# Sharing the last expert rows between two engines, and a new order of the first queries

## The reference

```python
def one_block(xb):                       # 128 tokens
    q = (xb @ wq).reshape(n, 8, 2, 64)                       # 8 heads of queries
    s = einsum('nhpk,pmk->nhpm', q, sub_keys)                # 2 x 128 scores per head
    sv, si = top_k(s, 16); cand_s = sv[0] + sv[1]; top_s, top_j = top_k(cand_s, 16)
    e = expert numbers of the 16 best;  g = softmax(top_s)
    act = gelu(einsum('nd,nhkd->nhk', xb, u[e]))             # u, v: 16384 rows of 1024 per layer
    return einsum('nhk,nhkd->nd', g * act, v[e])
```

## Time and profile before

| | us |
|---|---|
| median of three runs | 4258.71 |
| the three runs | 4248.27, 4258.71, 4259.67 |
| the profiled execution, its own time | 4255.55 |
| its span, first to last instruction | 4253.7 |
| PE busy / DVE / ACT / POOL in it | 3637.2 / 2550.2 / 963.9 / 2586.6 |
| moved by DMA | 1519.95 MB, 357 GB/s over the span |

### The profile page before, as it was taken

How to read it: one execution, slowest core, us unless ns; L and a number is a source line. 1 busy time by engine, 2 the same in 40 slices (tenths; PEclk the granted TensorE clock), 3 DMA queues, 4 the chain that set the end, 5 groups by cost and what they waited for, 6 DMA issues and landing times.

```text
span 4253.7 us, 37633 instructions
## 1 busy us (share of the span) xinstructions
PE 3637.2 (86%) x10554; PEld 1695.8 (40%) x10554; DVE 2550.2 (60%) x6442; ACT 963.9 (23%) x2490; POOL 2586.6 (61%) x2833
## 2 busy tenths in 40 slices
PE   7889899989988888888877899999898887777777
PEld 3354454545434223443332355554443432222222
DVE  1165456767665546566666555677676566666663
ACT  1212222222221112122222222222231122122121
POOL 0047446666665556676667663566676677777775
PEclk8899999999999999999999999999999999999999
DMA  6467889999999999999999988999999999999998
GB/s 240 160 237 270 283 325 391 360 392 403 361 366 383 376 383 354 351 362 351 400 396 409 354 291 298 364 369 389 394 407 350 368 401 406 407 406 405 401 402 325
DMA packets 472259, 1519.95 MB, mean 357 GB/s; under 512 B 59980, under 2 KB 78704, under 8 KB 471544
## 3 DMA queue, kind: packets, MB, share of 16 engines
q0 software_dynamic: 368640, 1342.34, 81.8%
q1 hardware_dynamic: 103416, 175.21, 11.6%
HBM read 1511.70 MB, written 5.67 MB: 357 GB/s over the span
## 4 chain that ended last, share of the span: by engine, by line
PE 44%; DMA 27%; POOL 13%; issue 9%; DVE 4%; ACT 2%; SPq 1%; DVEq 0%; ACTq 0%; POOLq 0%
PE expert_sum L2021 23%; DMA expert_rows<-in_peer_v,experts 23%; POOL expert_rows L989 11%; PE work L1780 4%; DMA expert_rows<-in_peer_u,experts 4%; PE work L1754 4%; PE work L1972 3%; PE work L1987 2%; PE work L1916 2%; PE work L1943 2%; PE work L1728 2%; DVE expert_rows L1697 1%; POOL stat_rstd L936 1%; PE work L1961 1%; PE work L1872 1%
## 5 line engine op out<-in xcount | busy, mean ns | idle before, releaser
L2021 PE MATMUL expert_sum<-expert_rows,weight_diagonals 128*128 128x512 f32 x5120 | 2481.8, 615 | 438.0 <-DMA expert_rows<-in_peer_v,experts 404.9
L1697 DVE CUSTOM_DVE_ANT_0 expert_rows<-expert_rows,tokens 128x1024 f32<-128x1024 f32 x1280 | 1556.7, 1216 | 846.1 <-DMA expert_rows<-in_peer_u,experts 832.1
L989 POOL DMA_INDIRECT expert_rows<-in_peer_v,experts x1280 | 1232.4, 963 | 921.6 <-PE expert_sum L2021 716.5
L2021 PEld LDWEIGHTS expert_sum<-expert_rows,weight_diagonals 128*128 128x128 f32 x5120 | 912.1, 193 | 1670.4 <-issue 1356.2
L989 POOL DMA_INDIRECT expert_rows<-in_peer_u,experts x1280 | 1219.5, 953 | 464.5 <-issue 348.4
L1263 ACT ACTIVATE weight_diagonals<-ident,expert_weights 128x128 f32<-128x128 f32 x1280 | 451.0, 392 | 600.6 <-PE expert_sum L2021 368.4
L1780 PE MATMUL work<-weight_ring,h_or_mixed 128*128 128x384 f32 (+3 forms) x800 | 252.7, 470 | 3.9 <-DMA weight_ring<-in_w_in 2.2
L1728 PE MATMUL work<-ident,scratch 128*128 128x128 f32 (+1 forms) x782 | 129.8, 289 | 93.3 <-DVE scratch L1355 35.5
L1780 PEld LDWEIGHTS work<-weight_ring,h_or_mixed 128*128 128x128 f32 x800 | 146.8, 194 | 110.2 <-issue 55.7
L1754 PE MATMUL work<-weight_ring,silu_cond 128*2 128x512 f32 x384 | 175.1, 610 | 12.5 <-DMA weight_ring<-in_w_mod 11.5
L1728 PEld LDWEIGHTS work<-ident,scratch 128*128 128x128 f32 (+1 forms) x782 | 99.0, 145 | 186.7 <-issue 72.5
(11 more groups left out here) (173 smaller groups left out, 2475.0 us busy)
## 6 DMA issues: line engine op xcount, KB each, us to landing
weight_ring<-in_w_mod SPq DMA_DIRECT2D x24, 2048.0 KB, 10.7
weight_ring<-in_w_out SPq DMA_DIRECT2D x16, 2048.0 KB, 19.1
weight_ring<-in_peer_wq SPq DMA_DIRECT2D x16, 2048.0 KB, 9.8
expert_rows<-in_peer_u,experts POOLq DMA_INDIRECT x1280, 7.3
expert_rows<-in_peer_v,experts POOLq DMA_INDIRECT x1280, 7.3
weight_ring<-in_w_in SPq DMA_DIRECT2D x12, 1536.0 KB, 8.0
weight_ring<-in_w_in SPq DMA_DIRECT2D x4, 2048.0 KB, 16.5
weight_ring<-in_t_pool SPq DMA_DIRECT2D x4, 2048.0 KB, 10.8
```

The costliest lines, as they stand in the source:

```text
L989: g.indirect_dma_start(ring[row % n], None, table, bass.IndirectOffsetOnAxis(ap=idx_st[:, col:col + 1], axis=0),).then_inc(row_in[row % n] ...
L1697: v_.tensor_tensor_reduce(out=u_ring[r % U_RING], in0=u_ring[r % U_RING], in1=tokens[:, :], scale=1.0, scalar=0.0, op0=ALU.mult, op1=ALU.a ...
L2021: ins = t_.matmul(acc[:, hf * 512:(hf + 1) * 512], diags[:, at * P:(at + 1) * P], v_ring[row % V_RING][:, hf * 512:(hf + 1) * 512], start= ...
```

## The change

There are two parts.

*At the end.* v rows 1260 to 1279 are shared: the odd ten are added by DVE into `block_sum` (the first by a `tensor_scalar`, nine by a `scalar_tensor_tensor` over 128 x 1024 floats), the even ten by PE as before. ACT makes diagonals for the even ones only. ACT's copy of the last block's sum is left out; in its place DVE adds `acc` and `block_sum`. The last 16 v rows use eight buffers: rows 1264 to 1267 and 1272 to 1275 the v ring, 1268 to 1271 and 1276 to 1279 the u ring, which no u row needs any more. A gather waits for whoever used its buffer last, PE or DVE.

*At the start.* The order is now q0, scores 0, q1 to q4, the gate exponentials of unit 0 (a step of its own, `ge`), q5, q6, scores 1, q7, scores 2. Of `topk(1)` only the first nine pieces stand ahead of row 0; the rest of it and `topk(2)` are done at two pieces behind each row of unit 0. ACT's `gate_exp(1)` is done at row step 1. Scores 2 keep their bank until row 6 (before: row 0).

```diff
+SHARED_ROWS = ((ALL_ROWS - 20, ALL_ROWS),)
+def added_by_dve(row):
+    return row % 2 == 1 and any(a <= row < e for a, e in SHARED_ROWS)
+def shared_block(n):
+    return any(a // BLOCK_ROWS == n for a, e in SHARED_ROWS)
 ...
 def first_units(queries):
-    return queries[:1] + [("top", 0)] + queries[1:2] + [("top", 1)] + queries[2:3] + [("score", 2)] + queries[3:]
+    return (queries[:1] + [("top", 0)] + queries[1:5] + [("ge", 0)] + queries[5:7] + [("top", 1)] + queries[7:]
+            + [("score", 2)])
 ...
     if kind == "score":
-        return [(step, 1, ("row", 0))]
+        return [(step, 1, ("row", 6))]
 ...
+        v_turns = [[] for _ in range(V_RING + U_RING)]
+        for r in range(ALL_ROWS):
+            late = r - (ALL_ROWS - TOPK)
+            v_turns[r % V_RING + (V_RING if late >= 0 and late // V_RING % 2 else 0)] += [r]
+        v_place = {r: (i, no) for i, turns in enumerate(v_turns) for no, r in enumerate(turns)}
 ...
             def expert_row(r):                      # POOL
 ...
-                    gather(peer_v, v_ring, v_in, v_done, v)
+                    i, no = v_place[v]
+                    if no:
+                        pool.wait_ge(*v_done(v_turns[i][no - 1]))
+                    elif i >= V_RING:
+                        pool.wait_ge(u_done, ALL_ROWS - U_RING + i - V_RING + 1)
+                    gather(peer_v, v_buffer(v), v_fills(v), v)
 ...
             def expert_row(r):                      # ACT
 ...
-                if 0 <= r - DIAG_LAG < ALL_ROWS:
+                if 0 <= r - DIAG_LAG < ALL_ROWS and not added_by_dve(r - DIAG_LAG):
                     diagonal(r - DIAG_LAG)
+                if r == 1:
+                    gate_exp(1)
 ...
+                    if shared_block(n):
+                        return
 ...
-            def whole_topk(unit):
-                for _ in topk(unit):
-                    pass
+            ahead = [iter(())]
+            def first_topk(unit):
+                if unit == 0:
+                    for _ in topk(unit):
+                        pass
+                    return
+                ahead[0] = topk(unit)
+                for _ in range(9):
+                    next(ahead[0])
 ...
+            def add_row(row):
+                unit, k = divmod(row, TOPK)
+                col = unit % 2 * TOPK + k
+                first = added.no.get(row - 2) is None
+                if first and row >= BLOCK_ROWS:
+                    dve.wait_ge(*x_updated.done(("fin", row // BLOCK_ROWS - 1)))
+                dve.wait_ge(weights_ready, unit + 1)
+                dve.wait_ge(*v_landed(row))
+                if first:
+                    v_.tensor_scalar(block_sum[:, :], v_buffer(row), wgt[:, col:col + 1], None,
+                                     ALU.mult).then_inc(added.sem, 1)
+                    return
+                dve.wait_ge(*added.done(row - 2))
+                v_.scalar_tensor_tensor(out=block_sum[:, :], in0=v_buffer(row), scalar=wgt[:, col:col + 1],
+                                        in1=block_sum[:, :], op0=ALU.mult, op1=ALU.add).then_inc(added.sem, 1)
             def expert_row(r):                      # DVE
                 unit, k = divmod(r, TOPK)
-                if k == 0:
+                if r == 0:
+                    ahead[0] = itertools.chain(ahead[0], topk(2))
+                elif k == 0:
 ...
-                next(ahead[0], None)
+                for _ in range(2 if unit == 0 else 1):
+                    next(ahead[0], None)
+                past = r - V_LAG
+                if past >= 0 and added_by_dve(past):
+                    add_row(past)
+                n = past // BLOCK_ROWS
+                if past >= 0 and past % BLOCK_ROWS == BLOCK_ROWS - 1 and shared_block(n):
+                    for last in all_v_done(past):
+                        dve.wait_ge(*last)
+                    v_.tensor_tensor(block_sum[:, :], acc[:, :], block_sum[:, :], ALU.add).then_inc(sum_copied, 1)
 ...
                 row = r - V_LAG                     # PE
-                if 0 <= row < ALL_ROWS:
+                if 0 <= row < ALL_ROWS and not added_by_dve(row):
 ...
-                                        start=first == 0, stop=first == BLOCK_ROWS - 1)
-                    ins.then_inc(v_done, 1)
+                                        start=first == 0, stop=row == last_of_pe[n])
+                    ins.then_inc(summed.sem, 1)
```

More of the change, by code:

```diff
@@ L1 @@
+import itertools
 import numpy as np
@@ L730, in build @@
         u_in, v_in = family("u_row_in", U_RING), family("v_row_in", V_RING)
-        u_done, v_done, tokens_ready = sem("u_rows_done"), sem("v_rows_done"), sem("tokens_ready")
+        u_done, tokens_ready = sem("u_rows_done"), sem("tokens_ready")
+        pe_rows = [r for r in range(ALL_ROWS) if not added_by_dve(r)]
+        summed = Steps(sem("v_rows_summed"), pe_rows)
+        added = Steps(sem("v_rows_added"), [r for r in range(ALL_ROWS) if added_by_dve(r)])
         idx_ready, gelu_ready, weights_ready = sem("experts_ready"), sem("gelu_ready"), sem("expert_weights_ready")
@@ L766, in head_done, with v_buffer, v_fills, v_landed @@
             return attended.done(item)
+        v_turns = [[] for _ in range(V_RING + U_RING)]
[3 more added lines that the diff above has]
+        v_place = {r: (i, no) for i, turns in enumerate(v_turns) for no, r in enumerate(turns)}
+        def v_buffer(row):
+            i = v_place[row][0]
+            return v_ring[i] if i < V_RING else u_ring[i - V_RING]
+        def v_fills(row):
+            i = v_place[row][0]
+            return v_in[i] if i < V_RING else u_in[i - V_RING]
+        def v_landed(row):
+            i, no = v_place[row]
+            earlier = 0 if i < V_RING else ALL_ROWS // U_RING
+            return v_fills(row), 16 * (earlier + no + 1)
+        last_of_pe = [max(r for r in pe_rows if r // BLOCK_ROWS == n) for n in range(LAYERS * NB)]
+        def v_done(row):
+            return added.done(row) if added_by_dve(row) else summed.done(row)
+        def all_v_done(row):
+            last_pe = max(r for r in pe_rows if r <= row)
+            theirs = [r for r in added.no if r <= row]
+            return [summed.done(last_pe)] + ([added.done(theirs[-1])] if theirs else [])
         block = ctx.enter_context(nc.Block())
@@ L981, in rope_keys_of, with gather @@
                 rope(("ukv", l, b))
[L983 to L987, removed]
+            def gather(table, buffer, row_in, row):
                 col = row // TOPK % 4 * TOPK + row % TOPK
-                g.indirect_dma_start(ring[row % n], None, table,
+                g.indirect_dma_start(buffer, None, table,
                                      bass.IndirectOffsetOnAxis(ap=idx_st[:, col:col + 1], axis=0),
-                                     ).then_inc(row_in[row % n], 16)
+                                     ).then_inc(row_in, 16)
             def row_u(row):
@@ L995, in row_u @@
                     pool.wait_ge(idx_ready, row // TOPK + 1)
-                gather(peer_u, u_ring, u_in, u_done, row)
+                if row >= U_RING:
+                    pool.wait_ge(u_done, row - U_RING + 1)
+                gather(peer_u, u_ring[row % U_RING], u_in[row % U_RING], row)
             def expert_row(r):
@@ L1257, in diagonal @@
                 unit, k = divmod(row, TOPK)
-                if k == 0:
+                if k < 2:
                     sc.wait_ge(weights_ready, unit + 1)
-                if row >= DIAGS:
-                    sc.wait_ge(v_done, row - DIAGS + 1)
-                col, at = unit % 2 * TOPK + k, row % DIAGS
+                no = summed.at(row) - 1
+                if no >= DIAGS:
+                    sc.wait_ge(*summed.done(pe_rows[no - DIAGS]))
+                col, at = unit % 2 * TOPK + k, no % DIAGS
                 a_.activation(diags[:, at * P:(at + 1) * P], ident[:, :], ACT.Copy,
@@ L1284, in _ @@
                     "ck": latent_keys, "kp": values, "kv": key_squares, "kT": keys_turn, "pd": pooled,
-                    "s": exponentials, "pt": turn_probs, "ot": mixed_turn, "q": queries_evac, "top": gate_exp,
+                    "s": exponentials, "pt": turn_probs, "ot": mixed_turn, "q": queries_evac, "ge": gate_exp,
                     "row": expert_row}
@@ L1649, in topk @@
                 if unit >= 4:
-                    dve.wait_ge(v_done, (unit - 3) * TOPK)
+                    for last in all_v_done((unit - 3) * TOPK - 1):
+                        dve.wait_ge(*last)
                 v_.tensor_scalar(idx_st[:, of_unit(unit)], tk["flat"], float(layer * NEXP), None,
```

15 lines of the change are left out of this document (7 added, 8 removed).

## The result

| | before | after |
|---|---|---|
| median | 4257.34 us (5 runs, 4248.27 to 4259.67) | 4231.16 us (5 runs, 4227.63 to 4239.24) |
| ratio | | 0.9945, 95% interval [0.9932, 0.9959] |
| span of the profiled execution | 4253.7 us | 4229.4 us |

The change makes the kernel faster by 0.55%. Predicted were 4238 us in a range of 4226 to 4250.

What follows compares the result with a forecast made beforehand. ACT's waits for DVE's maxima bound the start, PE and the ring of four buffers the tail. Gains of 11.5 + 7 = 18.5 us off 4255.55 give 4237.0, moved towards the runs' median to 4238; range 4226 to 4250.

Steps and rivals of the forecast that it cites:

- What bounds the start: Before row 0: ACT waits 8.43 and 10.87 us for DVE's maxima, and only then may empty q1 and q2.
- Queries and tokens: Start, PE: queries at ACT's emptying pace of 1.79 us per head, tokens at 228.8 instead of 245.9, 17 us earlier.
- DVE's start: Start, DVE: scores of unit 1 0.3 us later, nine pieces by 232.2, row 0 at 232.6 instead of 245.90, 13.2 us earlier.
- Rows 0 to 16: First unit, DVE: six pieces cost 4.2 us, a vanished wait returns 2.6; 11.6 us gained at row 16.
- The middle unchanged: Row 16 to row 1260: moved only as a whole; a length change above 4 us would show the forecast wrong.
- The end: Last v rows: 8.9 us gained from freer gathers and last steps, less 2.2 for adds against POOL; 6.7, say 7.
- The pause of 1.6 us: Tail, POOL: one pause in issuing gathers, likely to fall there too, moving the last gather from 4229.7 to 4231.3.
- the hold by the adds: Tail: DVE's adds with two SBUF inputs hold POOL's gathers; cost between 0 and 6.6 us, taken as 2.2.
- A: Rival, tail: every add holds a gather for most of its 1.23 us, the end gains nothing; 4244, chance 0.15.
- B: Rival, first unit: two pieces per row leave DVE behind by row 10, start gains 5; 4244, chance 0.12.
- C: Rival, tail: v gathers without u land at some 300 GB/s, the end gains 4; 4241, chance 0.08.
- D: Rival, slower: scores 2 keeping a bank until row 6 shifts later placements, 0.4 us per score; some 4272, chance 0.05.

Runs made afterwards that it cites:

- order_only: Kernel before with only the new order of queries and ACT's gate exponentials, unit 1's top-k still all ahead of row 0; 4242.2 us, ratio 0.9966.
- after_again: The changed kernel, unedited, measured and profiled once more; 4232.9 us, ratio 0.9947 to the kernel before.
- sum_in_psum: Changed kernel with DVE's running sum of the last v rows in the PSUM tile of the tokens instead of SBUF; 4233.6 us, ratio 0.9953.
- ring_by_turns: Changed kernel with DVE's sum in PSUM and, from row 1260 on, v and u buffers taking turns; 4235.4 us, ratio 0.9948.
- shared_four: Changed kernel with the last 20 v rows shared by DVE and PE, but in the four v buffers only; 4244.2 us, ratio 0.9973.
- end_alone: Changed kernel with the start part undone, so only the end part against the kernel before; 4251.6 us, ratio 0.9982.

## Why the prediction was right

*What bounds the start: right.* ACT's wait held q1 and q2, and through them PE, the tokens and row 0. order_only shows it by itself. The sign that I named came only in part: unit 1's exponentials still waited 5.29 us, more than the 1 us given, but behind the queries.

*Queries and tokens: right.* Expected 228.8 for the tokens; counted from the first query (20.5 us behind it) they were ready after 19.3. The pace of 1.79 us took PE's full clock for granted, and PE had it.

*DVE's start: 13.2 us earlier expected, 14.1 measured* (16.1 less the 2.0 before the first query). The scores of unit 1 were there before DVE wanted them, so nothing was lost there.

*Rows 0 to 16: the term that was mis-sized.* I charged the six last pieces at 4.2 us, as they stood alone, and credited only the 2.6 us wait for the first projection, keeping the others as a cushion. The charge was about right, even a little low: 3.2 us more busy time and 1.6 us more of short gaps, 4.8. The credit was wrong: the waits shrank by 5.4 us, from 6.8 to 1.4, for those for DMA and for POOL's statistics went too. The net is a gain of 0.5 us, not a loss of 1.6, and the start gained 14.7 us in this pair instead of 11.5. Against the mean of all profiles (13.2) half of that miss is scatter. The bend that I expected is there: the shift falls from 16.1 us at row 0 to 12.4 at row 11 and is back at 16.7 at row 16. It jumps back by 3.1 us at row 12, the one whose gather was waited for before.

*The middle unchanged: right*, to 0.05 us in the two profiles compared, which is luck given its scatter. The change of over 4 us that I named as the sign of being wrong came in after_again (3924.4, 5.9 us longer), with the same kernel: it was no sign of anything here.

*The end: 7 expected, 7.8 measured (8.5 in the means).* Counted from the product of u row 1279, the release of the first four gathers came out to 0.2 us. The pause of 1.6 us did not fall into the tail, the hold by the adds was 2.4 us (2.2 expected), and the landing took 6.1 us instead of 5.2. The last term rests on a wrong idea: the landing was not a fixed latency that the tail would keep. It took 6.1, 7.1 and 7.7 us where the last gather went 24.8, 22.6 and 22.3 us behind the mark (after, after_again, sum_in_psum). That the end came out so near is partly luck: a pause that stayed away paid for the longer landing. And the size of the hold was luck too, for it was 0.3 us in the same kernel the next time.

The Trainium skill (SBUF — State Buffer, "Who interferes with whom") has it that DVE with two SBUF inputs contends with a GpSimd instruction that reads SBUF, and that with at most one, outside DVE's two-port modes, it doesn't. Both halves agree with these runs: four gathers held by 0.1 to 1.0 us with two inputs, none of seventeen with one. The reservation counts too: in the changed kernel eight gathers that began 0.14 or 0.15 us behind the start of a `tensor_scalar` from SBUF to SBUF (L1411, 128 x 1024 floats in 0.75 us, one such input) took 1.48 to 1.50 us. As to the question left open, whole lengths are not lost, only what is left of the DVE instruction.

*Rivals.* A (the adds lock POOL out): the mechanism is real, its price at most about 1 us, not 8.6. B (DVE bound by row 10): the backlog is real and is given back by row 13. C (gathers alone don't reach 405 GB/s): false as a limit, for they do in sum_in_psum and ring_by_turns; but the changed kernel itself moved only 327 GB/s from 4196 to 4208, not the 400 that I named as a sign. (The sum of C is off by 1 us: 16 rows at 1.75 us from 4210.4 end at 4238.4.) D: excluded at its size.

The measured 4231.2 is 6.8 us under the 4238 forecast. In the profiled pair the start gave 3.2 us more than forecast and the end 0.8; the rest lies before the first query and in scatter.

## What to carry to other kernels

An in-order engine that holds a small waiting instruction ahead of other engines' supplies stalls them all; put that instruction behind what does not need it. Split the work of the engine that is then the last one, and in that order: the second step alone gave nothing. At the end of a stream, where one kind of transfer stops, its buffers are free: here more buffers and a second adder paid together (7.8 us), not singly (2.2 and 1.1). Once gathers are issued fast enough, the transfer itself is the limit: an earlier start of the free gathers took 4.5 us off this tail, taking the hold off them 1 us at most.

## What the hardware showed unasked

Taking work off PE can end in a granted clock at half level, and needn't. In shared_four PE was busy for 4.70 of the ten us from 4192 to 4202 and fell to 0.5 at 4204.0; a row's sum then took up to 3.75 us instead of 1.95. In the profile of the changed kernel it was as idle (5.87 of the twelve us from 4196 to 4208) and stayed at 1.00; in after_again, the same kernel, it fell. Of the seven profiles with shared rows three show a fall in the tail (after_again, end_alone, shared_four), of the six without none. What decides is not shown.

The middle of this kernel, 3.9 ms with gathers, varies by 18 us between profiled executions (3915.6 to 3933.3) with its code unchanged but for a bank. The clock goes with it: the profiles with a middle of 3926 us or more have a mean granted clock of 0.969 to 0.972, those up to 3924 have 0.971 to 0.976. Whether the clock is the cause or follows from PE's longer waits was not tested.
